# Layer 0's experts in 24 blocks instead of 25, with one fixed expert and five shared groups, in another order of blocks and weight buffers

## What is computed

```
expert = gi[:, None] * MOE_EPG + ti                  # two experts of one group per token
gate, up = jnp.split(h_pad[idx] @ w_gu[e], 2, axis=-1)
y = (jax.nn.silu(gate) * up) @ w_down[e]             # for the tokens idx of expert e
out = zeros.at[slot_tok].add(y * slot_w)             # summed over the two experts
```

## Time and profile before

| | us |
|---|---|
| median of 3 executions | 2719.36 (2715.66 to 2719.83) |
| the profiled execution | 2719.59 |
| its span | 2717.3 |
| PE busy, DVE, ACT, POOL | 2623.4, 1051.5, 553.1, 268.5 |
| HBM read and written | 555 MB and 46 MB, 221 GB/s |
| mean granted clock of PE | 0.983 |

### The profile page before, as it was taken

The page is one execution under the profiler, slowest core; times in us unless marked ns, Lnnn a source line. Parts: engine busy times, 40 slices in busy tenths (PEclk is TensorE's granted clock), DMA queues, the critical chain, the costliest instruction groups (busy, mean ns, idle before and its releaser), DMA issues.

```text
span 2717.3 us, 34118 instructions
## 1 busy us (share of the span) xinstructions
PE 2623.4 (97%) x13452; PEld 1324.1 (49%) x13452; DVE 1051.5 (39%) x2446; ACT 553.1 (20%) x1153; POOL 268.5 (10%) x366
## 2 busy tenths in 40 slices
PE   7999999998999999999999899899999999999997
PEld 3444456555755544433333354477755444443442
DVE  3222327106745642222222375577745611111114
ACT  3201111116721100000000131288821100000002
POOL 0011200003001110000000003000011100000002
PEclk8999999999999999999999999899999999999998
DMA  9651110206060279999999930300041699999996
GB/s 381 237 191 34 36 39 28 74 0 122 2 235 31 93 268 422 427 376 407 395 379 370 353 133 1 65 6 2 1 158 62 237 373 424 417 422 404 414 422 253
DMA packets 99722, 590.70 MB, mean 217 GB/s; under 512 B 21694, under 2 KB 24982, under 8 KB 74600
## 3 DMA queue, kind: packets, MB, share of 16 engines
q1 hardware_dynamic: 81672, 535.72, 50.4%
q0 software_dynamic: 15296, 43.31, 4.1%
q10 hardware_dynamic: 2592, 9.44, 0.9%
HBM read 554.98 MB, written 45.99 MB: 221 GB/s over the span
## 4 chain that ended last, share of the span: by engine, by line
PE 89%; DMA 7%; DVE 2%; issue 1%; SPq 1%; POOL 0%; ACT 0%; POOLq 0%; DVEq 0%; ACTq 0%
PE PS L2058 34%; PE PS L984 20%; PE PS L1689 9%; PE PS L1500 4%; PE PS L1512 4%; PE PS L1523 4%; PE PS L1169 4%; DMA ar<-in_expert_w_gu_dram 3%; PE PS L2063 1%; DMA ar<-in_ada_w_dram 1%; PE PS L613 1%; PE PS L2068 1%; PE PS L1708 1%; PE PS L1664 1%; PE PS L866 1%
## 5 line engine op out<-in xcount | busy, mean ns | idle before, releaser
L2058 PE MATMUL PS<-ar 128*32 128x512 f32 (+2 forms) x4608 | 1012.1, 596 | 17.2 <-DMA ar<-in_expert_w_gu_dram 11.3
L2058 PEld LDWEIGHTS PS<-ar 128*32 128x32 f32 (+2 forms) x4608 | 372.1, 137 | 620.2 <-issue 612.8
L984 PE MATMUL PS<-ar 128*128 128x512 f32 (+1 forms) x1344 | 566.0, 578 | 4.6 <-DMA ar<-in_swa_w_in_dram 3.0
L984 PEld LDWEIGHTS PS<-ar 128*128 128x128 f32 x1344 | 253.3, 192 | 282.3 <-issue 275.9
L1689 PE MATMUL PS<-ar 128*128 128x512 f32 x576 | 256.0, 599 | 0.6 <-DVEq L442 0.6
L2196 ACT ACTIVATE ar<-PS 128x512 f32<-128x512 f32 x48 | 28.7, 597 | 1064.5 <-PE PS L2058 1064.5
L1554 DVE CUSTOM_DVE_ANT_0 ar<-PS,ar 128x640 f32<-128x640 f32 (+2 forms) x208 | 158.0, 797 | 205.4 <-POOL ar L1470 133.5
L1689 PEld LDWEIGHTS PS<-ar 128*128 128x128 f32 x576 | 107.8, 192 | 123.6 <-issue 122.8
L1609 ACT ACTIVATE ar<-ar 128x641 f32<-128x641 f32 (+4 forms) x208 | 159.5, 772 | 2.2 <-DVE ar L1554 2.2
L2268 DVE TENSOR_TENSOR ar<-PS,ar 128x512 f32<-128x512 f32 x48 | 33.2, 692 | 316.8 <-ACT ar L2196 316.8
L2291 DVE TENSOR_TENSOR ar<-PS,ar 128x1024 f32<-128x1024 f32 x48 | 58.8, 1225 | 242.3 <-PE PS L2058 137.1
(11 more groups left out here) (290 smaller groups left out, 1956.4 us busy)
## 6 DMA issues: line engine op xcount, KB each, us to landing
ar<-in_expert_w_gu_dram SPq DMA_DIRECT2D x128, 2048.0 KB, 16.5
ar<-in_expert_w_down_dram SPq DMA_DIRECT2D x64, 2048.0 KB, 15.6
ar<-in_ada_w_dram SPq DMA_DIRECT2D x24, 2048.0 KB, 13.7
ar<-yd SPq DMA_DIRECT2D x36, 512.0 KB, 5.7
ar<-in_ab_w_in_dram SPq DMA_DIRECT2D x7, 2048.0 KB, 8.8
h2d<-ar ACTq DMA_DIRECT2D x18, 512.0 KB, 2.6
ar<-mod SPq DMA_DIRECT2D x3, 1536.0 KB, 7.8
ar<-in_x_dram SPq DMA_DIRECT2D x8, 512.0 KB, 13.3
```

The lines of the kernel that those rows point to most:

```text
L984: mm = nc.tensor.matmul(out_, lhs, rhs, start=(k == 0), stop=(k == KC - 1))
L2058: mm = nc.tensor.matmul(out[at:to], lhsT[:, at:to], w[:, k, cols], start=start, stop=stop)
```

## The change

Layer 0 has one fixed expert (`FIXED = (1, 2)`), three pairs, five groups of three and five singles: 1 + 3 + 15 + 5 = 24 blocks. Their order is: the fixed one; then a single ahead of each pair; the five groups one after another; two singles. The slots per expert (64 in a pair, 96 in a group, 128 alone) stay. Layer 1 stays as it was (its counts and order are written in another way). The order of loads and buffers changes with it:

- The first three loads are gate, up and down of expert 0, in buffers 2, 1 and 0 (`ring`); all others wait for `r0_ord`.
- The last load is put into buffer 0.
- PE runs up(0) before turn(1), since the rows of block 1 are now gathered with the sorted table.
- The four late loads of `ada_w` go to other buffers and wait for other products: up of the last block but one, down of the last but two, gate and up of the last, where they waited for gate, up, up of the last and down of the last but one.

The diff, without the constants of `C_KEY`, `rank_short`, `route_first`, `route_shift` and `route_slots`, in which `2` becomes `FIXED[l]`:

```diff
 FF = 512
 TOPK = 2
 OVF = 2 * TOK // P
-PAIRS, SHARED, MAINS = (3,9),(4,0),(3,0)
+PAIRS, SHARED, MAINS, FIXED = (3, 9), (5, 0), (3, 0), (1, 2)
 NOROW = 4096
 NLOG = GRP + EXP
 EPS = 1e-6
...
 
     a, b, c = rank_bounds(l)
     short = [0, 64, P - 32 * MAINS[l], 32, 0]
-    return [(at, short[i] - short[i + 1]) for i, at in enumerate((2, a, b, c)) if short[i] != short[i + 1]]
+    return [(at, short[i] - short[i + 1]) for i, at in enumerate((FIXED[l], a, b, c)) if short[i] != short[i + 1]]
 
 
 def moe_blocks(l):
 
     pairs, shared, mains = PAIRS[l], SHARED[l], MAINS[l]
     a, b, c = rank_bounds(l)
+    fixed = FIXED[l]
     whole = lambda r, col: dict(parts=[(r, 0, P)], col=col)
-    first = [whole(0, 0), whole(1, 1)]
-    groups = [[dict(parts=[(2 + 2 * i, 0, 64), (3 + 2 * i, 64, P)], col=2 + i)] for i in range(pairs)]
-    groups += [[dict(parts=[(b + mains * i + j, 0, 96), (a + i, 96, P)], col=2 + pairs + mains * i + j) for j in range(mains)]
+    first = [whole(r, r) for r in range(fixed)]
+    groups = [[dict(parts=[(fixed + 2 * i, 0, 64), (fixed + 1 + 2 * i, 64, P)], col=fixed + i)] for i in range(pairs)]
+    groups += [[dict(parts=[(b + mains * i + j, 0, 96), (a + i, 96, P)], col=fixed + pairs + mains * i + j) for j in range(mains)]
                for i in range(shared)]
-    rest = [whole(r, 2 + pairs + shared * mains + r - c) for r in range(c, EXP)]
+    rest = [whole(r, fixed + pairs + shared * mains + r - c) for r in range(c, EXP)]
+    if l == 0:
+        seq = first
+        for i, group in enumerate(groups):
+            seq = seq + rest[i:min(i + 1, pairs)] + group
+        return seq + rest[pairs:]
     seq = first + groups[0]
     for i in range(1, len(groups)):
         seq += rest[(i - 1) * len(rest) // (len(groups) - 1):i * len(rest) // (len(groups) - 1)] + groups[i]
-    if l == 1:
-        seq[-2:] = [seq[-1], seq[-2]]
+    seq[-2:] = [seq[-1], seq[-2]]
     return seq
 
 
...
                 self.blocks, self.pieces, self.at, self.fills = moe_blocks(l), [], {}, [0] * 6
                 nb, known = len(self.blocks), {}
                 for b in range(nb + 1):
-                    for part, k in (("g", b), ("d", b - 1), ("u", b)) if l == 1 and b == nb - 1 else (("g", b), ("u", b), ("d", b - 1)):
-                        if not 0 <= k < nb:
+                    order = (("g", b), ("u", b), ("d", b - 1))
+                    if l == 1 and b == nb - 1:
+                        order = (("g", b), ("d", b - 1), ("u", b))
+                    if l == 0 and b == 0:
+                        order = (("g", 0), ("u", 0), ("d", 0))
+                    for part, k in order:
+                        if not 0 <= k < nb or (l == 0 and b == 1 and part == "d"):
                             continue
                         for r, lo, hi in self.blocks[k]["parts"]:
                             if (part, r) not in known:
...
                         return -1
                     x = self.pieces[held[q]]
                     return dict(g=4 * x["last"], u=4 * x["last"] + 1, d=4 * x["last"] + 6)[x["part"]]
+                ring = (2, 1, 0, 3, 4, 5) if l == 0 else range(6)
                 for i, x in enumerate(self.pieces):
-                    q = min(range(6), key=lambda q: (free_at(q), q))
+                    q = min(ring, key=lambda q: (free_at(q), ring.index(q)))
+                    if l == 0 and i == 3 * EXP - 1:
+                        q = 0
                     self.fills[q] += 1
                     x.update(buf=q, fill=self.fills[q], freed=held[q])
                     held[q] = i
...
                     f = self.pieces[x["freed"]]
                     sp.wait_ge(*done(f"{self.n}_" + dict(g="ga", u="gu", d="dn")[f["part"]], f["last"] + 1))
                 r = x["rank"]
-                e = r if r < 2 else sp.value_load(ord_i[0:1, r:r + 1], min_val=0, max_val=EXP - 1)
+                e = r if r < FIXED[self.l] else sp.value_load(ord_i[0:1, r:r + 1], min_val=0, max_val=EXP - 1)
                 weight_load(sp, self.l, x["part"], e, self.buf(i)).then_inc(S(f"{self.n}_w{x['buf']}"), 16)
 
             def weights(self, pe, part, b):
...
 
 
         ADA, EARLY = 12, 10
-        lateada = [[R(piece_at[q], 4096).rearrange("p (k n) -> p k n", k=4) for q in pair] for pair in ((2, 3), (5, 4))]
+        lateada = [[R(piece_at[q], 4096).rearrange("p (k n) -> p k n", k=4) for q in pair] for pair in ((4, 5), (3, 2))]
         laterow = [R(ROWS + 2048 + 256 * i, 256) for i in range(2)]
         adaw = [[R(a, 4096).rearrange("p (k n) -> p k n", k=4) for a in pair] for pair in ((10240, 20480), (25600, 29696))]
         modrow = [ar[:, a:a + 256] for a in (24576, 25088)]
...
         def ada_late_load(sp, moe):
 
             nb, n = len(moe.blocks), moe.n
-            for part, b, i, h in (("ga", nb, 0, 0), ("gu", nb, 0, 1), ("gu", nb, 1, 0), ("dn", nb - 1, 1, 1)):
+            for part, b, i, h in (("gu", nb - 1, 0, 0), ("dn", nb - 2, 0, 1), ("ga", nb, 1, 0), ("gu", nb, 1, 1)):
                 sp.wait_ge(*done(f"{n}_{part}", b))
                 l, j = ada_of(EARLY + i)
                 sp.dma_start(lateada[i][h], A["ada_w"][l].rearrange("(p k) n -> p k n", k=KC)[:, 4 * h:4 * h + 4, j * D:j * D + D])\
...
                     route_shift(pe, l)
                 if b >= 1:
                     turn_gu(b - 1)
+                if l == 0 and b == 0:
+                    up(0)
                 if b + 1 < nb:
                     turn(b + 1)
-                up(b)
+                if l == 1 or b >= 1:
+                    up(b)
                 if b >= 1:
                     down(b - 1)
             if l == 1:
...
                     pool.wait_ge(*done(f"{n}_tr", b - 1))
                 c = moe.blocks[b]["col"]
                 pool.indirect_dma_start(out=hb[b % 2], out_offset=None, in_=h2d,
-                                        in_offset=bass.IndirectOffsetOnAxis(ap=(first_i if b < 2 else src_i)[:, c:c + 1], axis=0),
+                                        in_offset=bass.IndirectOffsetOnAxis(ap=(first_i if b < FIXED[l] else src_i)[:, c:c + 1], axis=0),
                                         bounds_check=TOK - 1, oob_is_err=False)\
                     .then_inc(S(f"{n}_hb{b % 2}"), 16)
 
...
                                         bounds_check=2 * TOK - 1, oob_is_err=False).then_inc(S(f"{n}_yo{b % 2}"), 16)
             pool.wait_ge(*done(f"o{l}_h2o", 16 * tiles_of(l)))
             pool.wait_ge(*done(f"r{l}_first", 1))
-            gather(0)
-            gather(1)
+            for b in range(FIXED[l]):
+                gather(b)
             pool.wait_ge(*done(f"r{l}_idx", 1))
-            for b in range(2, nb):
+            for b in range(FIXED[l], nb):
                 gather(b)
                 if b >= 4:
                     scatter(b - 4)
...
             moe, n = Moe(l), f"m{l}"
             nt = tiles_of(l)
             sp.wait_ge(*done(f"o{l}_mm", 2 * nt))
-            for i in (3, 4):
-                moe.load(sp, i)
+            if l == 1:
+                for i in (3, 4):
+                    moe.load(sp, i)
             sp.wait_ge(*done(f"o{l}_h2", 2 * nt))
             sp.wait_ge(*done(f"r{l}_ord", 1))
-            for i in range(5, len(moe.pieces)):
+            for i in range(3 if l == 0 else 5, len(moe.pieces)):
                 moe.load(sp, i)
                 if i == 6:
                     sp.wait_ge(*done(f"o{l}_r", nt))
```

More of the change, by code:

```diff
@@ L61 @@
 C_KEY = C_SL + P
-C_N = C_KEY + 32
+C_N = C_KEY + 64
 def rank_bounds(l):
     pairs, shared, mains = PAIRS[l], SHARED[l], MAINS[l]
-    a = 2 + 2 * pairs
+    a = FIXED[l] + 2 * pairs
     return a, a + shared, a + shared + shared * mains
@@ L131, in tables @@
     c[:, C_SL:C_SL + P] = np.arange(P)
-    c[:, C_KEY:C_KEY + 32] = np.arange(32) - np.where(np.arange(32) < 2, 1e6 * (2 - np.arange(32)), 0)
+    for l in range(2):
+        c[:, C_KEY + 32 * l:C_KEY + 32 * l + 32] = np.arange(32) - np.where(np.arange(32) < FIXED[l], 1e6 * (2 - np.arange(32)), 0)
     inv = (np.float32(10000.0) ** (-np.arange(16, dtype=np.float32) / np.float32(16))).astype(np.float32)
@@ L1943, in route_shift @@
             if PAIRS[l]:
-                mm = nc.tensor.matmul(PS[64:128, 7, 0:a - 2], cst[:, C_ID:C_ID + 64], Vp[:, 2:a], start=True, stop=True)
+                f = FIXED[l]
+                mm = nc.tensor.matmul(PS[64:128, 7, 0:a - f], cst[:, C_ID:C_ID + 64], Vp[:, f:a], start=True, stop=True)
             for j in range(MAINS[l]):
@@ L1961, in route_slots @@
             if np_:
-                V.tensor_copy(Vb[0:64, 2:at], two(Vp[0:64, 2:a])[:, :, 0])
+                V.tensor_copy(Vb[0:64, f:at], two(Vp[0:64, f:a])[:, :, 0])
             if ns:
@@ L1967, in route_slots @@
             if np_:
-                last = V.tensor_copy(Vb[64:128, 2:at], two(PS[64:128, 7, 0:2 * np_])[:, :, 1])
+                last = V.tensor_copy(Vb[64:128, f:at], two(PS[64:128, 7, 0:2 * np_])[:, :, 1])
             if ns:
```

7 lines of the change are left out of this document (4 added, 3 removed).

## The result

The changed kernel took **2728.66 us** in the median of seven runs (2723.95 to 2733.84), the kernel before 2717.39 beside it (2714.94 to 2720.85): ratio **1.0040**, 95% interval 1.0028 to 1.0052, so 11.3 us slower. The forecast was 2725.8. The profiled execution took 2729.30 us, its span is 2727.5. The same kernel, measured again later with nine runs, gave 2727.41 and 1.0035 (1.0025 to 1.0045).

The account below looks back on a forecast made before the run. PE sets the time in layer 0's experts, with the weight ring within 2 us of doing so. Terms -22.3 + 7.4 + 2.4 + 8.8 + 1.7 + 10.0 - 1.6 = +6.4 us, about 2725.8 us; range 2709 to 2737.

Parts of the forecast that it names:

- 4 blocks 1 to 6: Layer 0 blocks 1 to 6: same loads and waits as before, only shifted, with the 1.87 us wait: 0.
- 5, 6 clock in the stage: Lower PE clock after block 7's wait of 4.1 us in layer 0: +1.7 us.
- Steps 1 to 3: Layer 0: one block less -22.3 us; start waiting for block 1's gather +7.4; lower clock after that wait +2.4.
- Step 5: Block 7, now opening a group: waits for weight loads of 2.3, 2.4 and 4.1 us, +8.8.
- Step 6: Groups one after another: a 2.5 us weight wait at blocks 10, 13, 16 and 19, +10.0 us.
- every wait halves it: Rival: the six new waits of 2.3 to 2.5 us also cost 1.7 us of clock each, +10.2, 2736.0; chance 0.10.
- Step 7: End of layer 0: removed modulation wait worth 0, last scatter shortens from 7.15 to 5.5 us, -1.6 (0 to -2.2).
- one of the prediction's own signs: Sign of being wrong: the part behind 1560 us moves by other than the stage does.
- Step 8: Layer 1: order unchanged, 32 more columns of constants are 16 KB once: 0.
- the ring: Layer 0's six weight buffers, filled in turn: one load per 5.5 us in a full queue, so PE waits for weights.
- the ring keeps up: Rival: loads leave the queue every 4.9 us, the groups' waits vanish, -12.1 us, 2707.3; chance 0.13.

Follow-up runs that it names:

- the halved loads: Kernel before and changed kernel, each with half of every layer 0 weight load from the seventh on: 2904.71 us (1.0696) and 2886.98 us (1.0630).
- The start alone: The change's start (one fixed expert, up(0) ahead of turn(1)) in 25 blocks without the new order, against the kernel before: 2723.91 us, 1.0030.
- the order alone: Kernel before with 25 blocks and its own start, only reordered: four groups one behind the other after the pairs, five singles last: 2732.78 us, 1.0065.
- mix b: 24 blocks with groups, pairs and singles mixed for even demand, plus six filler matmuls in the start, against the kernel before: 2714.41 us, 0.9986.

## Why the prediction was right, and where it was not

| term | forecast | first trace | second |
|---|---|---|---|
| 1 one block less | -22.3 | -22.3 (a block's period; -23.1 by the halved loads) | -22.3 |
| 2 start, gate(1) - gate(0) | +7.4 | +7.6 | +7.7 |
| 3 clock there, to up(1) | +2.4 | +2.1 | +1.6 |
| 4 blocks 1 to 6 | 0 | -0.7 | -1.9 |
| 5 block 7: waits | +8.8 | +7.3 | +7.7 |
| 6 blocks 10 to 19: waits | +10.0 | +15.0 | +12.3 |
| 5, 6 clock in the stage | +1.7 | +8.5 | +3.4 |
| stage | +8.0 | +17.7 | +9.5 |
| 7 behind the last down, to layer 1's first product | -1.6 | -4.6 | -4.5 |

(The measured terms of the stage add to 17.5 and 8.5. The prediction expected the last down product to end near 1539; it did at 1548.8 and 1539.6.)

- **Steps 1 to 3** came as worked out: the gather landed after 10.5 us where I took 11.0, PE stood 6.03 for 6.6, gate(1) began at 991.51 for 991.6. The start alone cost 9.0 in the stage for 9.8.
- **Step 5** had the places and the largest wait (2.40 and 4.00 for 2.3 and 4.1); the middle one was 0.62 for 2.4, because the gate before it ran 1.70 us longer at the lower clock. The three products began at 1131.42, 1142.38 and 1153.46, as their loads landed, so the four loads from the first to the third came in 22.0 us: the interval of 5.5 us per load, seen again.
- **Step 6** had the mechanism, and the size was low. I took one wait of 2.5 us per group, at the first up. Part of the miss is a slip: midway between 7.7 and 10.9 is 9.3 and not the 9.0 I used, and with 9.3 each group would wait about 0.3 us more. The first trace has the wait in two pieces, at the first gate and the first up, in three of four groups, 2.9, 3.8, 1.9 and 2.8 us; and it has waits for down loads (2.21 and 1.40) of which my sketch had none. From up(10) to up(19) a group took 73.0 us in the first trace and 70.3 in the second, against 66.9 for PE alone; my forecast is 69.4. The rate across the groups was 382 and 396 GB/s, not the 410 to 420 that I expected. So full engines alone do not account for the waits; loads that can be issued only late, when one of the six buffers comes free, fit as well. How much either gives is open: halving the loads eases both, and a ring of more buffers was not run.
- **The clock** is the term that was most mis-sized: one halving forecast in the stage, five and two seen, 8.5 and 3.4 us for 1.7. I let only the 4.1 us wait cost clock, and made "every wait halves it" a rival of 0.10. Neither is what the chip does; for waits of about 2 us it is now one, now the other. "HAM oscillation" in the Trainium skill, "TensorE: Matmul & The Clock Gate", which I quoted for that rival, has a loop fall at each of its waits; the trace agrees for the 4 us wait and not for that of 2.04 us at 1218.
- **Step 7** was wrong in size and lay outside its own range (0 to -2.2). I bounded the scatter below by the quiet gather of 4.9 us; alone it took 3.27. And "the removed wait is worth 0" held only for PE: what the earlier late loads gave came through the chain beside it. Putting the placement back to one like the old cost 4.3 us. By one of the prediction's own signs it was wrong here: the part behind the stage moved otherwise than the stage, by 7.2 us.
- **Step 8**: from layer 1's first product to the end the first trace is 2.5 us shorter than before. Other kernels with the same code there lie from 1159.3 to 1163.7 us; not explained, and within that spread.

The two misses, too little for waits and clock in the stage and too little gain behind it, have opposite signs and partly cancel, and the median came out 11.3 (then 10.5) us above before for 6.4 forecast. The time itself, 2728.66 for 2725.8, is nearer than that by luck: the 2719.36 from which I counted, of three executions, was 2.0 above the 2717.39 of seven. The sign rested on the ring, by which the rival "the ring keeps up" was set aside. The runs confirm it from both sides: the order alone loses 16.8 us in the stage, and with half the bytes the change gains 14.3. The gather took what the rows said. By the rule of "DMA: Bandwidth & Descriptors" in the Trainium skill, section "Queues, rings and completion order", round-robin packet by packet, it should have landed within some 5 us beside the loads, an estimate from that rule. The traces do not agree: it took 10.3 to 14.2 there, and 4.4 when nothing stood in the queue.

## What to carry to other kernels

Where two resources are near full, a saving on one is worth only what the other leaves: first write down how many bytes each stretch asks for in how many microseconds of the engine, and compare that with the rate of a stretch whose queue is never empty. If the mean fits and a stretch doesn't, reorder so that heavy and light stretches alternate; that gave 9 to 14 us here, with the same 96 loads and 24 blocks. And when loads are moved to an earlier freed buffer, look at the last small transfer on the chain beside them, not only at the engine that waited for them.

## What the runs showed of the hardware

- **Waits and the clock.** Between block 1 and the last block of twelve traced executions PE stood 94 times for weights for 0.35 us or more (all runs above but those with halved loads). None of the 51 waits under 1.9 us was followed by a lower granted clock, 16 of the 33 from 1.9 to 2.6 us were, and 9 of the 10 longer ones (2.8 to 4.0); the clock then was at 1.2 GHz for 3.4 us, twice for 6.8. In one and the same program the number changes from one execution to the next: five such stretches, then two.
- **One program, several times.** The kernel before ran from 2714 to 2721 us, the change from 2720 to 2734; its stage differed by 8.2 us between two executions, of which the halvings explain 5.1 and the waits 3.0. Fewer waits do not always go with less spread: mix b, with 5.1 us of waits, ran from 2707 to 2718. One trace is one of these executions, so differences of stages below some 8 us between two single traces prove little; the medians carry the verdicts.
- **Small transfers beside large ones.** The first gathers of the stage, 0.5 MB each, took 4.4 to 5.7 us in a queue without loads, 7.8 with one load of 2 MB on its way (before), and 10.3 to 14.2 in the changed start with several; the last scatter, 0.5 MB, took 3.27 without and 5.76 to 8.19 with late loads beside it.
